# Forty feed-forward output tiles whose high weights meet both parts of a row in one matmul of 512 columns

## What is computed

```
def swiglu(x, w_in, w_out):
    a, gate = jnp.split(x @ w_in, 2, axis=-1)
    return (jax.nn.silu(a) * gate) @ w_out
...
    x = layer_norm(ALPHA * x + 0.5 * swiglu(x, w['ffn_w_in'][l, 0], w['ffn_w_out'][l, 0]), g[0], b[0])
```

## Time and profile before

| | |
|---|---|
| median of 3 runs | 2293.94 us (2288.88 to 2294.08) |
| the profiled execution | 2294.35 us, of which the span from first to last instruction is 2292.6 |
| TensorE busy | 2235.5 us, 98% of the span |
| VectorE busy | 1513.2 us, 66% |
| ScalarE busy | 1157.3 us, 50% |
| GpSimd busy | 575.3 us, 25% |

### The profile page before, as it was taken

One profiled execution on the slowest core, in us unless ns is written; L12 is line 12 of the kernel. 1 busy time (PEld: TensorE's weight loads), 2 busy tenths in 40 slices (PEclk: granted clock), 3 DMA queues, 4 the chain that ended last, 5 costly groups with the idle time before them and its releaser, 6 DMA issues.

```text
span 2292.6 us, 42675 instructions
## 1 busy us (share of the span) xinstructions
PE 2235.5 (98%) x17171; PEld 2198.6 (96%) x17171; DVE 1513.2 (66%) x2264; ACT 1157.3 (50%) x1951; POOL 575.3 (25%) x491
## 2 busy tenths in 40 slices
PE   8999999999998999999999999999999999999997
PEld 8999999999998999999999999999999998999997
DVE  5998868657799578444574585655687665475444
ACT  4444543656645558333364475555466554364332
POOL 2277301223111233111251132011452011131110
PEclk9999999999999999999999999999999999999998
DMA  9678665465676455555578655444555456355552
GB/s 245 173 224 233 202 215 161 144 173 152 201 226 189 134 145 169 181 149 149 172 225 249 188 160 179 141 121 139 164 153 179 130 151 190 110 159 165 144 155 83
DMA packets 705366, 391.13 MB, mean 171 GB/s; under 512 B 25001, under 2 KB 693138, under 8 KB 705170
## 3 DMA queue, kind: packets, MB, share of 16 engines
q1 hardware_dynamic: 662720, 332.44, 50.4%
q10 hardware_dynamic: 42450, 55.96, 7.0%
HBM read 366.53 MB, written 21.82 MB: 169 GB/s over the span
## 4 chain that ended last, share of the span: by engine, by line
PE 79%; DVE 4%; issue 3%; POOL 2%; ACT 1%; POOLq 0%; ACTq 0%; DVEq 0%
PE tile_ps L545 24%; PE tile_ps L547 23%; PE tile_ps L546 23%; PE misc L1751 1%; PE misc L1731 1%; DVE wl L523 1%; PE misc L2117 1%; POOL zq L889 1%; PE misc L2142 1%; PE misc L2317 1%; ACT wh L517 1%; PE misc L1748 1%; DVE r L981 0%; PE misc L2295 0%; POOL zc L772 0%
## 5 line engine op out<-in xcount | busy, mean ns | idle before, releaser
L523 DVE TENSOR_TENSOR wl<-raw,wh 128x1024 fp32r<-128x1024 f32 (+1 forms) x640 | 796.1, 1244 | 433.5 <-ACT wh L517 431.1
L545 PE MATMUL tile_ps<-xh,wh 128*128 128x256 f32 (+1 forms) x3520 | 1049.8, 298 | 17.4 <-DVE wl L523 6.8
L546 PE MATMUL tile_ps<-xl,wh 128*128 128x256 f32 (+1 forms) x3520 | 1033.1, 293 | 0.0
L547 PE MATMUL tile_ps<-xh,wl 128*128 128x256 f32 (+1 forms) x3520 | 1033.1, 293 | 0.0
L517 ACT CAST wh<-raw 128x1024 fp32r<-128x1024 f32 (+1 forms) x640 | 654.8, 1026 | 718.7 <-PE tile_ps L547 664.0
L545 PEld LDWEIGHTS tile_ps<-xh,wh 128*128 128x128 f32 x3520 | 664.0, 189 | 25.2 <-issue 8.4
L546 PEld LDWEIGHTS tile_ps<-xl,wh 128*128 128x128 f32 x3520 | 663.3, 188 | 0.9
L547 PEld LDWEIGHTS tile_ps<-xh,wl 128*128 128x128 f32 x3520 | 663.6, 189 | 0.0
L733 POOL TENSOR_TENSOR hl<-hf,hh 128x256 fp32r<-128x256 f32 (+1 forms) x176 | 243.4, 1383 | 1243.4 <-ACT hh L641 1242.5
L545 PE MATMUL tile_ps<-hh,wh 128*128 128x320 f32 (+1 forms) x1472 | 441.2, 300 | 1.9 <-DVE wl L523 1.8
L546 PE MATMUL tile_ps<-hl,wh 128*128 128x320 f32 (+1 forms) x1472 | 433.3, 294 | 0.0
(11 more groups left out here) (302 smaller groups left out, 1769.1 us busy)
## 6 DMA issues: line engine op xcount, KB each, us to landing
raw<-in_ffn_w_in_dram SPq DMA_DIRECT2D x352, 512.0 KB, 3.9
raw<-in_ffn_w_out_dram SPq DMA_DIRECT2D x128, 448.0 KB, 3.7
raw<-in_ffn_w_out_dram SPq DMA_DIRECT2D x64, 512.0 KB, 4.1
raw<-in_ssm_w_glu_dram SPq DMA_DIRECT2D x32, 512.0 KB, 3.8
raw<-in_attn_w_kv_dram SPq DMA_DIRECT2D x32, 512.0 KB, 3.9
wt<-scr_w ACTq DMA_DIRECT2D x16, 512.0 KB, 4.7
cp<-scr_c ACTq DMA_DIRECT2D x16, 512.0 KB, 4.6
raw<-in_attn_w_q_dram SPq DMA_DIRECT2D x16, 512.0 KB, 3.9
```

What stands on the lines that cost most here:

```text
L523: nc.vector.tensor_tensor(wl[n % RAWS][:, 0:k, :], raw[n % RAWS][:, 0:k, :], wh[n % WS][:, 0:k, :].bitcast(F32), ALU.subtract).then_inc(w_ ...
L545: nc.tensor.matmul(o, wh[w][:, kk, :], xa, start=kk == 0, stop=False)
L546: nc.tensor.matmul(o, wh[w][:, kk, :], xb, start=False, stop=False)
L547: return nc.tensor.matmul(o, wl[n % RAWS][:, kk, :], xa, start=False, stop=kk == ROWS[n] - 1)
```

## The change

In five "out" stages of h = 0, named in `WIDE`, the two products with `wh` become one matmul. `hh` and `hl` are now two halves of one buffer, `h_both`, so that a row's high and low part can be read as one operand of 2 x 256 columns. The wide matmul writes the high product into columns 0 to 255 of the bank and the low product into columns 256 to 511; the third matmul adds wl x high to the first half. For each of these 40 tiles VectorE adds the first half to `r` as before, makes the low weights, and then adds the second half, and only this second add gives the bank back. The rest of the kernel is as it was.

```diff
+WIDE = ((2, 0, 0), (2, 0, 1), (2, 0, 2), (3, 0, 0), (3, 0, 1))
+WIDE_TILES = {FIRST["out", _f, _h, _p] + _d for _f, _h, _p in WIDE for _d in range(DT)}
...
-        hh = keep("hh", [P, KMAX, NMAX], F32R)
-        hl = keep("hl", [P, KMAX, NMAX], F32R)
+        h_both = keep("h_both", [P, 2, KMAX, NMAX], F32R)
+        hh, hl = h_both[:, 0], h_both[:, 1]
...
+        def pe_row_wide(n, kk):
+
+            o, w, N = ps[:, n % PSS, :], n % WS, NT[0]
+            nc.tensor.matmul(o.rearrange("p (a n) -> p a n", a=2), wh[w][:, kk, :], h_both[:, :, kk, 0:N],
+                             start=kk == 0, stop=False)
+            return nc.tensor.matmul(o[:, 0:N], wl[n % RAWS][:, kk, :], hh[:, kk, 0:N],
+                                    start=False, stop=kk == ROWS[n] - 1)
+
         def pe_row(n, h, hi, lo, kk):
+            if n in WIDE_TILES:
+                return pe_row_wide(n, kk)
...
+        s_wide = sem("wide_high_products_added")
+
+        def dve_add_wide(dve, f, h, p, beside):
+            for d in range(DT):
+                n, N = FIRST["out", f, h, p] + d, NT[h]
+                dve.wait_ge(tile_done, n + 1)
+                nc.vector.scalar_tensor_tensor(out=r[:, d, CS[h]], in0=r[:, d, CS[h]], scalar=1.0 if p else ALPHA,
+                                               in1=ps[:, n % PSS, 0:N], op0=ALU.mult, op1=ALU.add).then_inc(s_wide, 1)
+                dve_lo(dve, n + WS)
+                dve.wait_ge(s_wide, DT * WIDE.index((f, h, p)) + d + 1)
+                nc.vector.tensor_tensor(r[:, d, CS[h]], r[:, d, CS[h]], ps[:, n % PSS, N:2 * N], ALU.add
+                                        ).then_inc(drained[n % PSS], 1)
+                step(beside)
+
         def dve_out(dve, f, h, p, beside=None):
+            if (f, h, p) in WIDE:
+                dve_add_wide(dve, f, h, p, beside)
+                return
             dve_add(dve, ("out", f, h, p), h, 1.0 if p else ALPHA, beside)
```

## The result

The kernel after takes 2297.3 us (median of 14 runs, 2295.41 to 2301.19), the kernel before 2292.88 (14 runs, 2288.88 to 2294.48). The ratio is 1.0021, with a 95% interval of 1.0014 to 1.0028: the change costs about 4.8 us, between 3.2 and 6.4. That is inside the 0.3% that the forecast called "no difference", but it is 5 us above the 2292.3 us that was predicted, 0.3 us outside the range, and on the other side of zero.

A forecast was written before the change was run, and what follows sets the result against it. TensorE's stream of matmuls was taken to bound the kernel. Rows (-2.6 us) and longer fold waits (+1.0) made -1.6 us, giving 2292.75 from the profiled 2294.35, or 2292.3 us against the median of 2293.94; range 2286.8 to 2297.0.

The forecast's parts named there:

- no difference: Whole kernel: a change within about 0.3% (6.9 us), which a measurement can't tell from none; chance 0.85.
- the sum's first term: Rows of the five wide stages: 344.5 ns each, 8.9 ns less; 296 rows save 2.6 us.
- the cost grows with the columns: Wide rows: matmul cost proportional to columns, 352.5 ns a row, 0.3 us saved, time 2294.6; chance 0.22.
- The bound from above: Wide rows: line through 256 and 320 columns gives 364.7 ns a row, so the rows lose 3.3 us.
- from below: Wide rows: bare streaming of 512 columns plus 113.3 ns gives 326.6 ns a row, saving 7.9 us.
- The hidden load: Wide rows: a long matmul hides its weight load entirely, 331.9 ns a row, time 2288.5; chance 0.20.
- The restart of the second piece: Wide matmul: its second 256-column piece costs a restart of 44 ns, time 2305.3; chance 0.05.
- The cover of the second add: VectorE's second add: covered in f = 2; in (3, 0, 1) it lengthens three folds' waits, 1.0 us more.
- The norm sums: GpSimd's sums in (2, 0, 2): start a little later, but later tiles lie over them; no cost counted.
- The pace of untouched tiles: 26 input and head tiles of f = 2: could fall from 113.3 to 117.8 ns, 2.8 us; shared chance 0.11.
- another mechanism: f = 3 stages: TensorE waits 0.42 us in each of 16 tiles for VectorE, time 2298.0; shared chance 0.11.
- The sum: Whole kernel: -2.6 us from rows and +1.0 us of waiting make -1.6 us.

The follow-up runs named there:

- in turns: Kernel after with extra matmuls of alternating widths, 16 repeats each, ahead of the seventh tile of (2, 0, 1); 512 + 256 took 353.3 ns, total time not given.
- the ladder: Kernel after with 24 extra matmuls per width, 64 to 512 columns, ahead of the seventh tile of (2, 0, 1); total time not given.
- the break: Kernel after with two plain 128-column matmuls opening the first input tile of (2, 0, 2); 2300.59 us in one run.
- f = 3 only: Kernel after with only the two stages (3, 0, 0) and (3, 0, 1) wide, 16 tiles of 40; 2294.56 us, ratio 1.0007.
- f = 2 only: Kernel after with only the three stages of f = 2 wide, 24 tiles of 40; 2294.7 us, ratio 1.0009.

## Why the prediction was wrong

**The step that failed** is the sum's first term: one load runs under the wide matmul, "and it costs what one load costs under the nearest wide neighbour, 13.4 ns", so "344.5 ns per row", 8.9 ns less, and 2.6 us in 296 rows. The row measures 353.4 ns in the kernel (19.79 us / 56) and 353.3 in turns. The three wide stages of f = 2 gained 0.14 us, and (3, 0, 0) 0.08. Two things were wrong in that step. The wide matmul repeated alone costs 15.4 ns over streaming at its best, not 13.4 (228.7 ns; the ladder), which would still have left 6.9 ns a row. And in the row it doesn't reach this: it steps by 233.7 ns there, 20.4 over streaming, and the narrow matmul behind it by 119.7. What one load costs is thus no fixed piece that can be carried over from 320 columns. The rival "the cost grows with the columns" gave 352.5 ns a row and came nearest in size, and its 234.7 ns are near what the wide matmul takes in the row. But its reason is wrong, so this is luck: by rate, 192 columns would take 88 ns and take 111.7, and 384 columns 176 and take 173.3. The bound from above, 364.7, and from below, 326.6, did hold it.

**The hidden load** (0.20) is refuted: 15.4 ns or more over streaming at 512 columns. The fp32 records on which it leaned, two cycles a column, don't carry over to one cycle a column. (The four of rows 8 are two matmuls, as line 2295 issues two; the profile has two records for each.) **The restart of the second piece** (0.05) is refuted outright: 5.75 us with and without.

**The cover of the second add.** The step was "three folds' waits", 0.26 + 0.35 + 0.35 = 1.0 us. The place, the engine and the cause were right (without the add the folds are as before). The size was 1.80 us for the stage, of which the three folds take 0.28 + 0.69 + 0.76. The first was right to 0.02. In the other two I followed the add in the same tile and not the one of the tile before, which delays the steps of the sample head whose result comes back through ScalarE ahead of the same maxima. The run with the add behind the work beside shows this by taking one of the two away.

**The norm sums** were costed at nothing, since "the 8 tiles of k and 16 input tiles of the other half lie over them". They cost 0.33 to 0.35 us. Timeline of the kernel after, VectorE, GpSimd and TensorE at the end of (2, 0, 2):

```profile
1329.70 0.41 DVE L723 TENSOR_TENSOR r<-r,tile_ps 128x256 f32<-128x256 f32 x1
...
1330.19 0.74 POOL L803 TENSOR_TENSOR zc<-zc,r 128x256 f32<-128x256 f32 x1 [1.72 <-DVE r L723]
...
1330.98 0.70 PE L815 MATMUL misc<-zc,ones 128*128 128x256 f32 x2
```

The last second add stands behind the weights in VectorE's list, so GpSimd's last sum starts at 1330.19, and TensorE's reduction of it, which stands *in* TensorE's list one tile into k, waits for it. Before, GpSimd's sum came 2.3 us earlier against the tiles. Later tiles don't cover a matmul that stands ahead of them in the same list; I had looked at what follows and not at where the waiting instruction stands.

**The pace of untouched tiles** stood among the rivals, with 2.8 us for 26 tiles and a chance of 0.11 shared with another mechanism. It happened to 20 of the tiles: +1.27, +0.72 and +0.09 us. My argument against it, that the pace changed "at the very tiles at which the operand changed", was wrong: the same tiles with the same operand run at either pace, and the break gives the faster one back. Of the +1.27 it is shown that one wide stage ahead is enough, that it goes without one, and that a break ends it; the run of the ladder, where two wide tiles ahead don't bring it, shows that this is not the whole cause. Of the +0.72 in (2, 0, 0) only this is shown: it is there or not by the program, among those profiled, it doesn't need wide tiles ahead, and the kernel before doesn't have it. Whether to call it a cost of the change is open.

**The sum** with the measured terms: -0.4 (rows and small rests) + 1.8 (folds) + 0.3 (norm sums) + 2.1 (pace) = +3.8 us, where -1.6 was forecast, and 4.8 (3.2 to 6.4) were measured. The forecast also stood on a median of three runs, 1.06 us above that of 14. The medians can't check the split: f = 3 only and f = 2 only lie 0.9 and 1.8 us above their own runs of before, 2.6 together, each with an interval of some 2 us to either side. No version that computes the same came out below the kernel before; one whose wide rows keep the pace of 349 ns was not found.

What stays open: what picks the pace of 512 columns (228.7 or some 233.5 ns) and so that of the row (349 or 353.3); what picks the pace of 256 columns; and the +0.72.

## What to carry to other kernels

A price per instruction that is read from a stream of equal instructions doesn't hold in a mixed one: before building on it, run the exact pattern beside the old one for 16 turns; here that would have shown 353.3 against 353.3 ns. Leave the first turns out, and look for a second pace before taking the number as fixed. For an operation that is added to an engine's list, follow it into every chain that passes through that engine, also those that go out to another engine and come back, and count each copy of it that stands ahead of the waiting instruction. And judge cover by where the waiting instruction stands in its own engine's list, not by how much work comes after it.

## What the runs showed of the hardware that was not expected

- A matmul that loads 128 x 128 weights takes 111.7 ns at 64, 128 and 192 columns alike (the ladder).
- 256 columns run at 113.3 or at 117.8 ns at the same tiles of the program, and keep the pace over hundreds of matmuls (288 in (2, 0, 2)); two other matmuls between brought back the faster one. Which pace untouched tiles have also hangs on what else the program holds: 7 tiles of (2, 0, 0) and, in three of the experiments, 8 tiles of the queries. At 320, 384 and 448 columns it is 146.7, 173.3 and 199.9 ns.
- 512 columns repeated run at 228.7 or at 233.5 ns, and a row of 512 and 256 at 349.0 or 353.3.
- 512 columns read as two pieces of 256 cost the same as 512 adjoining ones, 228.7 ns.
- Stretches of 3.4 or 6.8 us at 1.2 GHz lie at a few places that come back, but each run of one program has its own choice of them. One at 2043.4 us cost 1.52 us. The runs of the kernel after with a mean granted clock of 0.992 took 2299.5 us in the median, those with 0.994 2296.9, so these stretches make much of the scatter. For differences of 1 to 4 us, the comparison of stages in two profiles was the sharper tool, and the medians of 11 runs the check on it.
